# The state-space stage with exponents summed in PSUM, and expert work laid out anew

## The reference

```
Lmat    = exp(where(i >= j, cs[i] - cs[j], -inf))
y_intra = sum over j of  (C_i . B_j) * Lmat[i, j] * dt[j] * x[j]
```

## Time and profile before

| | |
|---|---|
| median of 3 runs | 1485.54 us (1479.41 to 1486.49) |
| profiled execution, its own time | 1473.01 us |
| its span | 1471.0 us |
| TensorE matmul busy | 1275.7 us, 87% |
| VectorE busy | 642.9 us, 44% |
| ScalarE busy | 560.6 us, 38% |
| GpSimd busy | 172.2 us, 12% |
| mean granted TensorE clock | 0.95 of full speed |

### The profile page before, as it was taken

One profiled execution on the slowest core, in us unless ns is written; L12 is line 12 of the kernel. 1 busy time (PEld: TensorE's weight loads), 2 busy tenths in 40 slices (PEclk: granted clock), 3 DMA queues, 4 the chain that ended last, 5 costly groups with the idle time before them and its releaser, 6 DMA issues.

```text
span 1471.0 us, 18374 instructions
## 1 busy us (share of the span) xinstructions
PE 1275.7 (87%) x7648; PEld 971.2 (66%) x7648; DVE 642.9 (44%) x1109; ACT 560.6 (38%) x1084; POOL 172.2 (12%) x173
## 2 busy tenths in 40 slices
PE   6999499899899598777768899999789999899877
PEld 6888465677754433111128798888779889789777
DVE  1686746233970401000034244565665235455754
ACT  4445422222320220000026554544656563554552
POOL 0566631220720200000000000000000000000000
PEclk9999899999999699999998899999999989999989
DMA  5433324677006579999961416244332424415210
GB/s 181 154 133 116 114 82 142 234 254 261 1 17 269 201 309 423 421 421 421 421 266 47 169 58 210 81 145 142 115 104 79 148 99 173 143 59 183 103 58 29
DMA packets 90325, 256.98 MB, mean 175 GB/s; under 512 B 6606, under 2 KB 11239, under 8 KB 77827
## 3 DMA queue, kind: packets, MB, share of 16 engines
...
...
## 4 chain that ended last, share of the span: by engine, by line
PE 54%; DVE 13%; DMA 12%; ACT 11%; POOL 5%; issue 4%; SPq 1%; DVEq 0%; ACTq 0%
PE bank L680 52%; DMA ring<-in_w_up_dram 7%; DMA ring<-in_w_down_dram 4%; PE bank L689 3%; POOL late L2503 2%; POOL acc L2504 2%; DVE ring_r L1911 2%; ACT L1453 2%; ACT w_hi_r L1453 2%; DVE acc L1972 2%; ACT prob L1453 1%; DVE nmx L2358 1%; DVE prob L2355 1%; DMA ring<-in_w_ada_dram 1%; ACT xT L1453 1%
## 5 line engine op out<-in xcount | busy, mean ns | idle before, releaser
L680 PE MATMUL bank<-ring_r,xT_hi 128*128 128x256 f32 (+1 forms) x864 | 247.5, 286 | 0.0
L1911 DVE TENSOR_TENSOR ring_r<-ring,w_hi_r 128x1024 fp32r<-128x1024 f32 x136 | 161.9, 1222 | 163.8 <-ACT w_hi_r L1453 163.0
L680 PE MATMUL bank<-w_hi_r,xT_hi 128*128 128x256 f32 x704 | 209.6, 298 | 17.4 <-ACT gs L1453 7.4
L680 PE MATMUL bank<-w_hi_r,xT_r 128*128 128x256 f32 x704 | 203.3, 289 | 0.0
L680 PEld LDWEIGHTS bank<-ring_r,xT_hi 128*128 128x128 f32 x864 | 170.1, 197 | 0.2
L680 PEld LDWEIGHTS bank<-w_hi_r,xT_hi 128*128 128x128 f32 x704 | 138.5, 197 | 31.3 <-DVE ring_r L1911 17.8
L1453 ACT ACTIVATE w_hi_r<-ring 128x1024 fp32r<-128x1024 f32 x136 | 137.6, 1052 | 51.8 <-PE bank L680 50.7
L680 PE MATMUL bank<-ring,xsT 128*32 128x512 f32 x512 | 114.7, 594 | 30.8 <-DMA ring<-in_w_up_dram 16.6
L680 PEld LDWEIGHTS bank<-w_hi_r,xT_r 128*128 128x128 f32 x704 | 137.8, 196 | 0.0
L680 PE MATMUL bank<-xT,ring 128*128 128x256 f32 x576 | 127.2, 384 | 0.0
L680 PEld LDWEIGHTS bank<-xT,ring 128*128 128x128 f32 x576 | 110.9, 193 | 15.4
...
## 6 DMA issues: line engine op xcount, KB each, us to landing
...
```

Source lines behind the costliest of these rows:

```text
L680: return release(nc.tensor.matmul(o, lhsT, rhs, start=start, stop=stop))
L1911: tt(lo, raw_, hi.bitcast(F32), ALU.subtract).then_inc(lo_done.sem, lo_done.one("piece"))
```

## The change

- The running sums `gc` are split into a high and a low fp32r half (`halves_r`), transposed in the convolution stage, and kept as rows `gT_r` of 96 partitions. `hot_r` has a one at a column in both halves, so a one-pass product of `hot_r`'s column with `gT_r` writes a head's running sums to all 128 partitions. `kq_decay` uses this for two products of 256 columns in the place of four fp32 products.
- The logarithm of dt minus gc is kept as `lnd`; ScalarE takes the logarithm before `eg` and `ed`.
- The state-space stage's unit is now two heads with both chunks and both directions. `ssd_args(u)` writes per direction the mask and two heads' sums into a bank; `ssd_exps(u)` takes eight exponentials of 128x128 from the bank with `lnd` as the bias; `ssd_sum` adds the directions, one product with C.B (`cbs`, copied by ScalarE, unmasked) gives `W`; TensorE makes four products per unit. The subtraction, the minimum and the products with dt go. `xw` moves to GpSimd, one per round of the delta rule; the squares of the delta rule's output are taken per round.
- The bias strips are made one behind each block of expert group 1, the modulation gates in group 2. The memory of `bias` serves once as a sixth room, for the sixth expert block; the experts' outputs `ysb` move to `xn2` and `xT`, and `cT` is declared later so that `bias` doesn't lie on it.

```diff
-    slot = [n % 2 if n < n1 else (n - n1 + 2) % RING if n < n2 else (n - n2) % (RING - 1) for n in range(len(plan))]
+    slot = [n % 2 if n < n1 else RING if n == n1 + 5 else (n - n1 + (2 if n < n1 + 5 else 1)) % RING if n < n2 else (n - n2) % (RING - 1) for n in range(len(plan))]
...
-            cbm = tiles(0, 8).rearrange("p (g c d) n -> p g c d n", g=SG, c=TT)
-            df = [t.rearrange("p (d j) n -> p d j n", d=2) for t in (tiles(8, 8), ring[2][:, 0:1024].rearrange("p (i n) -> p i n", i=8))]
-            tm = [t.rearrange("p (d j) n -> p d j n", d=2) for t in (tiles(16, 8), ring[2][:, 1024:2048].rearrange("p (i n) -> p i n", i=8))]
+            cbs = tiles(0, 4).rearrange("p (g c) n -> p g (c n)", g=SG)
+            EE = [t.rearrange("p (d i) n -> p d (i n)", d=2) for t in (tiles(8, 8), ring[2][:, 0:1024].rearrange("p (i n) -> p i n", i=8))]
+            W = [t.rearrange("p (j c) n -> p j c n", j=2) for t in (tiles(16, 4), ring[2][:, 1024:1536].rearrange("p (i n) -> p i n", i=4))]
...
+        ring += (bias[:].rearrange("p h n -> p (h n)"),)
...
-            ysb = strips[:].rearrange("p h n -> p (h n)")[:, 0:NE // EG * D].rearrange("p (g n) -> p g n", g=NE // EG)
+            ysb = [xn2[:, t, :] for t in range(TT)] + [xT[:, t * DK // 2:(t + 1) * DK // 2, :].rearrange("p k n -> p (k n)") for t in range(TT)]
...
+                if n == 3:
+                    pe.wait_ge(front_dve.sem, front_dve.at("halves"))
+                    for c in range(TT):
+                        last = tr(bank[5][0:2 * NSC, c * P:(c + 1) * P], halves_r[:, c, :].bitcast(F32))
+                    last.then_inc(front_pe.sem, front_pe.one("rows"))
...
-                for c in range(TT):
-                    for d in range(2):
-                        i = 2 * c + d
-                        last = mm(bank[2 + h % 2][:, i * P:(i + 1) * P], g[:, c, d * GH + h:d * GH + h + 1].to_broadcast([P, P]),
-                                  TRI["fw" if d == 0 else "bw"], False, i == 3)
+                for d in range(2):
+                    col = d * GH + h
+                    last = mm(bank[2 + h % 2][:].rearrange("p (c d n) -> p d c n", c=TT, d=2)[:, d], hot_r[0:2 * NSC, col:col + 1].to_broadcast([2 * NSC, P]),
+                              gT_r[0:2 * NSC], False, d == 1)
...
+            def ssd_args(u):
+
+                if u >= 2:
+                    pe.wait_ge(ssd_exp.sem, u - 1)
+                for d in range(2):
+                    b = bank[1 + 3 * (u % 2) + d]
+                    mm(b[:], eye_r[:, 0, :], nmask_r[:, d, :].unsqueeze(1).to_broadcast([P, 2 * TT, P]), True, False)
+                    for j in range(2):
+                        col = 2 * GH + d * SH + 2 * u + j
+                        last = mm(b[:, j * T:(j + 1) * T], hot_r[0:2 * NSC, col:col + 1].to_broadcast([2 * NSC, P]),
+                                  gT_r[0:2 * NSC].rearrange("p c n -> p (c n)"), False, j == 1)
+                last.then_inc(ssd_arg_pe.sem, ssd_arg_pe.one("unit"))
+
+            ssd_args(0)
+            ssd_args(1)
...
-            def ssd_decay(u):
-
-                c, gi, half = u // 4, u // 2 % 2, u % 2
-                if u >= 2:
-                    pe.wait_ge(ssd_dif_dve.sem, ssd_dif_dve.at("dif", u - 2))
-                for d in range(2):
-                    for j in range(4):
-                        col = 2 * GH + d * SH + gi * 8 + half * 4 + j
-                        last = mm(q4(bank[1 + 2 * (u % 2) + d], j), g[:, c, col:col + 1].to_broadcast([P, P]),
-                                  TRI["fw" if d == 0 else "bw"])
-                last.then_inc(ssd_decay_pe.sem, ssd_decay_pe.one("decay"))
...
-            ssd_decay(0)
-            ssd_decay(1)
             for u in range(8):
-                c, gi, half = u // 4, u // 2 % 2, u % 2
                 b = u % 2
 
                 v, sd = u // 2, u // 2 % 2
                 if u % 2 == 0:
-                    pe.wait_ge(ssds_dve.sem, ssds_dve.at("xw"))
+                    pe.wait_ge(ssds_pool.sem, v + 1)
                     if v:
                         pe.wait_ge(ssdy_dve.sem, v)
-                    mm(bank[7][:], bnat[:, sd, v // 2 * P:(v // 2 + 1) * P], xw[v]).then_inc(ssds_pe.sem, ssds_pe.one("h"))
+                    mm(bank[3][:], bnat[:, sd, v // 2 * P:(v // 2 + 1) * P], xw[v]).then_inc(ssds_pe.sem, ssds_pe.one("h"))
                 else:
                     pe.wait_ge(ssds_act.sem, v + 1)
-                    mm(bank[7][:], cT[:, CT0 + v // 2, (1 - sd) * P:(2 - sd) * P], hst[v % 2]
+                    mm(bank[3][:], cT[:, CT0 + v // 2, (1 - sd) * P:(2 - sd) * P], hst[v % 2]
                        ).then_inc(ssds_pe.sem, ssds_pe.one("y"))
                 if u + 2 < 8:
-                    ssd_decay(u + 2)
-                pe.wait_ge(ssd_tm_dve.sem, ssd_tm_dve.at("tm", u))
+                    ssd_args(u + 2)
+                pe.wait_ge(ssd_w_dve.sem, u + 1)
                 if u >= 2:
                     pe.wait_ge(ssdo_dve.sem, u - 1)
-                for j in range(4):
-                    h = gi * 8 + half * 4 + j
-                    for d in range(2):
-                        last = mm(bank[5 + b][:, j * SP_:(j + 1) * SP_], tm[b][:, d, j, :], xnat[:, c, h * SP_:(h + 1) * SP_],
-                                  d == 0, d == 1)
+                for c in range(TT):
+                    for j in range(2):
+                        h = 2 * u + j
+                        last = mm(bank[6 + b][:, (2 * c + j) * SP_:(2 * c + j + 1) * SP_], W[b][:, j, c, :],
+                                  xnat[:, c, h * SP_:(h + 1) * SP_])
...
+                            if gi == 1:
+                                bias_strip(4 * pair + 2 * o + k0 // (DK // 2))
                         if pair:
                             last.then_inc(ex_pe.sem, ex_pe.one(("gate", "up")[o]))
                     if gi == 0 and pair == 0:
                         select_weights()
-                        bias_strips()
-                if gi == 0:
+                if gi == 2:
...
+                    f(lnd[:], lnd[:], ACT.Ln).then_inc(front_act.sem, front_act.one("lnd"))
...
+            def ssd_exps(u):
+
+                act.wait_ge(ssd_arg_pe.sem, u + 1)
+                if u >= 2:
+                    act.wait_ge(ssd_w_dve.sem, u - 1)
+                for d in range(2):
+                    for j in range(2):
+                        for c in range(TT):
+                            n, h = slice((2 * j + c) * P, (2 * j + c + 1) * P), d * SH + 2 * u + j
+                            last = f(EE[u % 2][:, d, n], bank[1 + 3 * (u % 2) + d][:, n], ACT.Exp, bias=lnd[:, c, h:h + 1])
+                last.then_inc(ssd_exp.sem, ssd_exp.one("unit"))
+
+            ssd_exps(0)
+            ssd_exps(1)
+            act.wait_ge(ssdh_pe.sem, 1)
+            f(cbs.rearrange("p g n -> p (g n)"), bank[0][:], ACT.Copy).then_inc(ssdh_act.sem, ssdh_act.one("cb"))
+            link(delta_squares(GH // 2 - 1))
...
-                act.wait_ge(ssd_min_pool.sem, u + 1)
-                f(df[u % 2], df[u % 2], ACT.Exp).then_inc(ssd_act.sem, 1)
                 if u % 2 == 0:
                     act.wait_ge(ssds_pe.sem, ssds_pe.at("h", u // 2))
-                    f(hst[u // 2 % 2], bank[7][:], ACT.Copy).then_inc(ssds_act.sem, 1)
+                    f(hst[u // 2 % 2], bank[3][:], ACT.Copy).then_inc(ssds_act.sem, 1)
+                if u + 2 < 8:
+                    ssd_exps(u + 2)
...
+            gh, gl = (halves_r[:, :, lo:lo + NSC] for lo in (0, NSC))
+            link(nc.vector.tensor_copy(gh, gc[:]))
+            tt(lnd[:], lnd[:], gc[:, :, 2 * GH:NSC], ALU.subtract)
+            tt(gl, gc[:], gh.bitcast(F32), ALU.subtract).then_inc(front_dve.sem, front_dve.one("halves"))
...
+                if n == 12:
+                    dve.wait_ge(front_pe.sem, front_pe.at("rows"))
+                    nc.vector.tensor_copy(gT_r[0:2 * NSC].rearrange("p c n -> p (c n)"), bank[5][0:2 * NSC, 0:T]
+                                          ).then_inc(front_dve.sem, front_dve.one("rows"))
...
-            ssd_dif(0)
-            for v in range(4):
-                gi, c = v // 2, v % 2
-                col = 2 * GH + c * SH + gi * 8
-                last = tt(xw[v].rearrange("p (h n) -> p h n", h=8),
-                          xnat[:, c, gi * 512:(gi + 1) * 512].rearrange("p (h n) -> p h n", h=8),
-                          dted[:, c, col:col + 8].unsqueeze(2).to_broadcast([P, 8, SP_]), ALU.mult)
-            last.then_inc(ssds_dve.sem, ssds_dve.one("xw"))
+            def ssd_sum(u):
+
+                dve.wait_ge(ssd_exp.sem, u + 1)
+                tt(EE[u % 2][:, 0], EE[u % 2][:, 0], EE[u % 2][:, 1], ALU.add).then_inc(ssd_sum_dve.sem, ssd_sum_dve.one("unit"))
+
+            ssd_sum(0)
+            dve.wait_ge(ssdh_act.sem, 1)
             for u in range(8):
-                c, gi, half = u // 4, u // 2 % 2, u % 2
-                if u < 7:
-                    ssd_dif(u + 1)
-                dve.wait_ge(ssd_act.sem, u + 1)
```

(26 more changed lines are left out.)

119 lines of the change are left out of this document (56 added, 63 removed).

## The result

The changed kernel took 1462.6 us (median of 4 runs, 1461.38 to 1467.1) where the kernel before took 1486.0 on the same chip (median of 4). The ratio is 0.9851, with a 95% interval of 0.9807 to 0.9895. It was timed a second time later, beside three other kernels: 1462.3 against 1482.0, ratio 0.9885 [0.9842, 0.9928]. One execution of the kernel before in that group took 4311.5 us and is left out throughout. The forecast was 1463.6.

The account below looks back on a forecast made before the run. No single engine was taken to bound the kernel; each stage was priced separately. Terms +2.2 - 3.6 + 1.0 - 12.6 - 8.9 = -21.9 us, taken from the median 1485.5, gave 1463.6, range 1452 to 1476.

Parts of the forecast that it names:

- The experts, -8.9: Expert blocks: closing the idle transfer hole saves 3.9 us, the sixth room one block of 4.98 us.
- Rival 2: Experts: the sixth block is worth nothing because a later slot stalls transfers once; 1468.6 us, chance 0.08.
- The state-space stage, -12.6: Delta rule's end to w_out: walked unit by unit, 15.1 us sooner, less deductions of 1.5 and 1.0; range -5 to -17.
- the deduction of 1.5 for contention: State-space stage: norm_delta on GpSimd slows VectorE's sums and products with both inputs in SBUF, costing 1.5 us.
- the prediction's own signs of being wrong: State-space stage: slower exponentials from a bank, or clock below 0.7 for over 10 us; projection: a wait on its first weights.
- Rival 1: State-space stage: VectorE and GpSimd lock each other out between 371 and 390; stage about -5, 1471 us, chance 0.13.
- Rival 3: State-space stage: ScalarE becomes the bound, exponentials at 0.6 us each; stage +7.4, 1483.6 us, chance 0.05.
- rival 4: Output projection: TensorE's clock stays at 1.2 GHz after the emptier state-space stage; up to 1519 us, chance 0.05.
- Decay masks, -3.6: Delta rule's masks: two one-pass products replace eight; 1.6 us for four warm heads, 2.0 for heads 2 and 3.
- Front, +2.2: Before VectorE's first tap: table load behind the logarithm, 1.28 + 0.2, and VectorE's small operations, 0.7; range 0.5 to 4.
- the price of the copy at tile 12: Convolution: VectorE's copy of transposed sums lies beside GpSimd's taps and costs nothing; uncovered, with the transposes, 0.5 us.
- Delta rule, +1.0: Delta rule: xw on GpSimd slows VectorE's r and u2, by nothing to 0.8 us a round; range 0 to +3.

Follow-up runs that it names:

- experiment 4: Changed kernel without GpSimd's four products that norm the delta rule's output, a memset in their place; 1461.9 us in one execution, state-space stage 37.4 us against 37.8.
- experiment 6: Changed kernel with ScalarE's logarithm and exponential for the delta rule's norm moved behind unit 3's exponentials; 1461.4 us in one execution, state-space stage 36.6 us.
- experiment 2: Changed kernel with the logarithm of the key's factor taken right behind the softplus's logarithm; 1456.6 us in one execution, copy of gc to first tap 3.11 against 4.67.
- experiment 3: Changed kernel with VectorE's copy of the transposed sums at tile 9 in place of tile 12; 1458.5 us in one execution, first tap to first mask 130.6.
- Experiment 1: The kernel before, unedited, profiled a second time; 1489.6 us, span 1487.5, which is 16.5 us over its first profile.

## Why the prediction was right, step by step

The forecast of 1463.6 is 1.0 us from the measured 1462.6. That closeness is in part luck: the interval of the ratio reaches from 15.6 to 28.7 us of gain, a second timing gave 19.7 in the medians, and the terms were off by up to 1.9 us each, in both directions. What held is the mechanism and the size of the two large terms.

- **The experts, -8.9: measured -8.7 to -9.0.** 4.9 from the sixth room (4.98) and 3.6 to 4.0 from the hole (3.9), each by its own experiment. One reading behind the term was wrong: the pieces of 18.35 us in the earlier trace rows are transfers from issue to landing, not waits of TensorE, which is busy 74.20 of 100 us there and waits at most 1.5 us at a time. That transfers bound the stage, at 421 GB/s, is right all the same, and the sum does not use the 18.4. Rival 2, that a slot stalls the transfers, is excluded: 222.1 against 217.2. The strips cost 0.91 and not 0.74, inside their cover of 1.50.
- **The state-space stage, -12.6: measured -14.2 and -14.4.** The term that was mis-sized is the deduction of 1.5 for contention: it is 0.4 (experiment 4). The walk without deductions put w_out 37.4 us behind the end of the delta rule's last product; the eight profiles that have the stage as the change made it show 37.1 to 39.1. The effect is larger for one instruction than assumed (2.85 for 0.69), but lies beside TensorE's products at the low clock, so that a deduction for each counts part of the same time twice. What the clock costs in all is not shown: between profiles it makes 1.9 us (experiment 6), but no run had the stage at full clock throughout with nothing else changed, so whether 1.0 was too much stays open. The rest of the surplus is in the walk's own steps: a pair of units at full clock takes 6.05 us in place of 6.3, and from the third state to w_out it is 8.6 in place of 9.5. One of the prediction's own signs of being wrong did come in: in the first profile the clock is at its low level for 10.2 us of the stage, and the stage was still shorter than forecast.
- **Rival 1**, lock-out, had the mechanism and not the price. The sum that starts at 389.44 beside GpSimd's product ends at 392.29, 0.55 us behind the product's end at 391.74; that at 384.83 ends at 387.21, 0.55 behind 386.66. So it does not run slowly, it waits for the whole of the other and then runs. Operations with one input in a bank (0.41 at 387.14) are untouched. The lock of the Trainium skill (SBUF — State Buffer, Who interferes with whom) agrees with these rows. The prediction counted the output among the operations that the rule would hold up; it has one input in a bank and was not. Only few sums meet a GpSimd product, and then while TensorE is no sooner ready.
- **Rival 3** falls with 0.27 for each exponential, **rival 4** with the granted clock of the projection, of which this is the first window of the changed kernel:

```profile
410.00:430.00 20.00, 19.41 (x46) 8.68 (x47) 11.57 (x10) 1.82 (x3) 0.00 (x0) 1.00 0.16 58
```

- **Decay masks, -3.6: measured -2.5 and -1.7.** A size. The warm loop is 4.18 for two heads, 4.05 forecast. The 2.0 for heads 2 and 3 at the low clock was the weak term: from head 2's key products to head 4's it is 6.05 us before and 5.49 in the changed kernel, 0.6 won. The products of g got shorter there, but the key products of head 2 take 2.08 in place of 1.35, since the clock is low for longer. The rest of the stage gave 1.9, 1.6 forecast.
- **Front, +2.2: measured +2.4**, of it 1.56 the load's new place (experiment 2). Wrong was the price of the copy at tile 12, called covered or 0.5: TensorE waits up to 4.37 us for it, which is worth 0 or 1.1 (experiment 3).
- **Delta rule, +1.0**: measured +1.1 and +0.4 in the first and second profiles against the first of before; the mean of 11 profiles with the new stage is 172.6 us, of 3 with the old one 171.5. The size is right by luck, for the reason given is not the one: VectorE's steps r and u2, beside GpSimd's xw, take what they took. Counted by rounds, from o to o, the mean of the new profiles against the old is +0.6 up to the first o, -0.4, +0.2 and +0.7 us. The last round takes 25.66 us in the three old profiles and 25.95 to 26.50 in the eleven new ones, and only in the new ones does TensorE wait in it for a block of modulation weights, 0.21 to 0.77 us. Timeline of TensorE in the last round, the kernel before and the second profile of the changed one:

```profile
355.88 1.92 PE L680 MATMUL bank<-ring,ccol 128*32 128x512 f32 x16
```

```profile
354.70 1.92 PE L680 MATMUL bank<-ring,ccol 128*32 128x512 f32 x16 [0.72 <-DMA ring<-in_w_ada_dram]
```

  So most of those 0.7 are a wait for a transfer. Why the weights come later against TensorE's work than before (the shorter masks may bring it there sooner) was not tested.
- **The base.** The sum was put on the median, not on the one profile, since "the terms don't depend on that". Experiment 1 bears this out: the profiled execution of the kernel before was a fast one behind the experts. From spans alone the change would look half as large as it is.
